# Routing and experts of a mixture-of-experts layer in one block, gate and up weights in four parts, the experts of a step packed in one integer

## What is computed

```python
g_idx = argmax(h @ w_group_router + b)            # one group per token
top_l, top_i = top_k(expert logits of that group, 2)
weights = p_g * softmax(top_l)
hidden = silu(h @ w_exp_gate[e]) * (h @ w_exp_up[e])
y += (hidden * weight) @ w_exp_down[e]            # for the token's 2 experts
x = x + gate2 * y ; out = rms_norm(x)
```

## Time and profile before

| | us |
|---|---|
| median of 3 runs (lowest, highest) | 1262.19 (1260.89, 1267.14) |
| the profiled execution | 1268.32 |
| its span, first to last instruction | 1266.5 |
| PE busy | 1106.8 (87%) |
| DVE busy | 580.6 (46%) |
| ACT busy | 428.6 (34%) |
| POOL busy | 228.4 (18%) |
| HBM read and written | 382.85 MB, 39.24 MB |

### The profile page before, as it was taken

One profiled execution on the slowest core, in us unless ns is written; L12 is line 12 of the kernel. 1 busy time (PEld: TensorE's weight loads), 2 busy tenths in 40 slices (PEclk: granted clock), 3 DMA queues, 4 the chain that ended last, 5 costly groups with the idle time before them and its releaser, 6 DMA issues. The chain is left out here.

```text
span 1266.5 us, 19400 instructions
## 1 busy us (share of the span) xinstructions
PE 1106.8 (87%) x7006; PEld 799.0 (63%) x7006; DVE 580.6 (46%) x1031; ACT 428.6 (34%) x853; POOL 228.4 (18%) x163
## 2 busy tenths in 40 slices
PE   4799999988999895988999799985899579799874
PEld 1587777767999795988888688885333123233241
DVE  0763554105456686777776376654111111111147
ACT  2651211113333772666667455520111001011112
POOL 0000000012000583467765000000100000000050
PEclk9899999999999997999999799987899889999978
DMA  9437676512200726254320533227577945757375
GB/s 354 145 115 252 219 259 223 177 45 72 55 1 1 185 74 157 37 124 103 85 67 1 186 100 104 97 68 276 206 242 233 324 167 194 273 163 237 134 259 205
DMA packets 126845, 196.87 MB, mean 155 GB/s; under 512 B 19504, under 2 KB 92112, under 8 KB 124702
## 3 DMA queue, kind: packets, MB, share of 16 engines
q1 hardware_dynamic: 116108, 162.22, 40.1%
q0 software_dynamic: 5760, 20.97, 4.9%
q10 hardware_dynamic: 4882, 12.44, 2.5%
HBM read 382.85 MB, written 39.24 MB: 333 GB/s over the span
## 5 line engine op out<-in xcount | busy, mean ns | idle before, releaser
L2145 PE MATMUL moe_gu_ps<-moe_wgu,moe_xT 128*32 128x512 f32 x1408 | 164.7, 609 | 25.2 <-DMA moe_wgu<-in_w_exp_up 24.6
L2145 PEld LDWEIGHTS moe_gu_ps<-moe_wgu,moe_xT 128*32 128x32 f32 x1408 | 45.7, 112 | 125.3 <-issue 124.2
L96 PE MATMUL proj_acc_ps<-proj_w_hi,hidden_hT_hi 128*128 128x512 f32 x288 | 117.5, 408 | 7.5 <-DVE hidden_hT_lo L91 7.5
L98 PE MATMUL proj_acc_ps<-proj_w_hi,hidden_hT_lo 128*128 128x512 f32 x288 | 114.3, 397 | 0.0
L97 PE MATMUL proj_acc_ps<-proj_w_lo,hidden_hT_hi 128*128 128x512 f32 x288 | 113.9, 396 | 0.0
L1322 POOL TENSOR_TENSOR att_e<-att_e 128x1152 f32<-128x1152 f32 (+1 forms) x36 | 86.0, 2389 | 72.9 <-DVE att_e L1402 72.9
L1340 ACT ACTIVATE att_e<-att_sc_ps,att_shift 128x1152 f32<-128x1152 f32 (+1 forms) x72 | 81.5, 1132 | 40.6 <-DVE att_shift L1391 40.4
L2167 PE MATMUL moe_y_ps<-moe_wd,moe_hidT 128*32 128x512 f32 x704 | 84.3, 621 | 11.4 <-issue 10.6
L1391 DVE TENSOR_REDUCE att_shift<-att_sc_ps 128x1 f32<-128x1152 f32 (+1 forms) x72 | 86.2, 1231 | 5.5 <-PE att_sc_ps L1436 5.5
L1465 PE MATMUL att_turned_ps<-att_in_v_tok,att_aT 128*128 128x128 f32 x584 | 76.9, 279 | 8.1 <-ACT att_aT L1348 8.1
L1465 PEld LDWEIGHTS att_turned_ps<-att_in_v_tok,att_aT 128*128 128x128 f32 x584 | 69.8, 191 | 13.7 <-ACT att_aT L1348 10.5
(11 more groups left out here) (372 smaller groups left out, 2102.3 us busy)
## 6 DMA issues: line engine op xcount, KB each, us to landing
moe_wgu<-in_w_exp_gate SPq DMA_DIRECT2D x178, 512.0 KB
moe_wgu<-in_w_exp_up SPq DMA_DIRECT2D x178, 512.0 KB
moe_wd<-in_w_exp_down SPq DMA_DIRECT2D x89, 1024.0 KB
scratch_y_slots<-moe_y ACTq DMA_DIRECT2D x22, 512.0 KB, 5.4
proj_raw<-in_w_in SPq DMA_DIRECT2D x32, 256.0 KB, 4.8
proj_feat<-in_w_ada SPq DMA_DIRECT2D x4, 2048.0 KB, 8.9
proj_xh<-in_w_ada SPq DMA_DIRECT2D x4, 2048.0 KB, 9.5
proj_feat<-in_w_ada SPq DMA_DIRECT2D x4, 1024.0 KB, 5.9
```

The costliest lines, as they stand in the source:

```text
L96: pe.matmul(out, a_high, b_high, start=start, stop=False)
L98: return pe.matmul(out, a_low, b_high, start=False, stop=stop)
L2145: mm = pe.matmul(gu_ps[n % 2][at, :], xT[:, n % 2, k * P + c * Q:k * P + (c + 1) * Q], wgu[:, c, k], start=(k == 0), stop=(k == KT - 1))
```

## The change

1. Routing and experts share one block and one scope for semaphores. The barrier between them and ACT's wait for the last h2 tile are gone; POOL waits for the token list (`tokens_done`) and the h2 tile (`h2_in`) before its first gather. To have room for both, the routing uses the experts' PSUM tiles and its one-hot matrices lie in the experts' `y` and `xT`; `xg` has two buffers instead of three.
2. Gate and up are loaded, waited for and released in four parts of 2 row tiles (256 KB a load) instead of two halves. The number of matmuls and their order are the same.
3. The codes of the four streams of a step are packed in one integer (5 bits each) by DVE; SP loads that once per step and takes experts and flags apart in registers, which are kept (`snap`).

```diff
+PARTS = 4
-def load_gate_up(sp, I, W, c, half, e, **cond):
-    rows = slice(half * (KT // 2), (half + 1) * (KT // 2))
+def load_gate_up(sp, I, W, c, part, e, new):
+    rows = slice(part * KT // PARTS, (part + 1) * KT // PARTS)
...
-def weights_of(eng, W, c, step):
-    n = c * STEPS + step
-    code = eng.value_load(W["block_weights"][0:1, n:n + 1], min_val=0, max_val=2 * NE - 1)
-    return code & (NE - 1), code >= NE
+def weights_of(eng, W, step):
+    code = eng.value_load(W["step_weights"][0:1, step:step + 1], min_val=0, max_val=(2 * NE) ** STREAMS - 1)
+    codes = [(code >> (5 * c)) & (2 * NE - 1) for c in range(STREAMS)]
+    return [(eng.snap(v & (NE - 1)), eng.snap(v >= NE)) for v in codes]
...
+        oh_place = [rows[:, 0:T * P].rearrange("p (t n) -> p t n", t=T) for rows in (spare_y, spare_x)]
+        x_ps, (rank_ps, sum_ps), table_ps, unread_ps = W["x_ps"], W["gu_ps"], W["h_ps"], W["y_ps"]
...
-            firsts = [weights_of(sp, W, c, 0) for c in range(STREAMS)]
-            for half in range(2):
-                sp.wait_ge(W["gu_in"][half], 16 * 2)
+            firsts = weights_of(sp, W, 0)
+            for part in range(PARTS):
+                sp.wait_ge(W["gu_in"][part], 16 * 2)
...
-            act.wait_ge(W["h2_in"], 16)
...
-            dve.scalar_tensor_tensor(out=W["block_weights"][0:1, :], in0=fresh[:]..., scalar=float(NE), in1=of_block[:]..., ...)
+            dve.scalar_tensor_tensor(out=codes[:], in0=fresh[:], scalar=float(NE), in1=of_block[:], op0=ALU.mult, op1=ALU.add)
+            dve.drain()
+            for c in range(STREAMS - 2, -1, -1):
+                dst = codes[:, c] if c else W["step_weights"][:]
+                op = dve.scalar_tensor_tensor(out=dst, in0=codes[:, c + 1], scalar=2.0 * NE, in1=codes[:, c], op0=ALU.mult, op1=ALU.add)
+                if c:
+                    dve.drain()
+            op.then_inc(blocks_done, 1)
...
-            dve.tensor_copy(W["step_token"][:], table_ps[:, 0:STEPS])
+            dve.tensor_copy(W["step_token"][:], table_ps[:, 0:STEPS]).then_inc(W["tokens_done"], 1)
...
-    XB = 3
+    XB = 2
...
+                now, ahead = ahead, weights_of(sp, W, n) if n < STEPS else []
+                for part in range(PARTS):
+                    sp.wait_ge(gu_done[part], n)
...
+            pool.wait_ge(W["tokens_done"], 1)
+            pool.wait_ge(W["h2_in"], 16)
...
-                pe.wait_ge(gu_in[half], gu_loaded(n))
-                for k in range(half * (KT // 2), (half + 1) * (KT // 2)):
+                for part in range(half * PARTS // 2, (half + 1) * PARTS // 2):
+                    pe.wait_ge(gu_in[part], gu_loaded(n))
+                    for k in range(part * KT // PARTS, (part + 1) * KT // PARTS):
...
+                    mm.then_inc(gu_done[part], 1)
...
-        routing_stage(nc, I, C, W, M)
+            block = moe_ctx.enter_context(nc.Block())
+            routing_stage(nc, I, C, W, M, block)
+            expert_stage(nc, I, C, W, M, block)
         late_ctx.close()
-        expert_stage(nc, I, C, W, M)
```

More of the change, by code:

```diff
@@ L2083, in expert_stage @@
         x_turned, x_left, x_right = s.sem("x_turned"), s.sem("x_left"), s.sem("x_right")
-        gu_done, silu_done, hid_done = [s.sem(f"gu_done{half}") for half in range(2)], s.sem("silu_done"), s.sem("hid_done")
+        gu_done, silu_done, hid_done = [s.sem(f"gu_done{part}") for part in range(PARTS)], s.sem("silu_done"), s.sem("hid_done")
         h_turned, hidT_done, d_done = s.sem("h_turned"), s.sem("hidT_done"), s.sem("d_done")
         y_left, y_right, y_out = s.sem("y_left"), s.sem("y_right"), [s.sem(f"y_out{u}") for u in range(2)]
-        block = ctx.enter_context(nc.Block())
         token, weight = W["step_token"], W["step_weight"]
@@ L2101, in _ @@
             for n in range(1, STEPS + 1):
-                now, ahead = ahead, [weights_of(sp, W, c, n) for c in range(STREAMS)] if n < STEPS else []
-                for half in range(2):
-                    sp.wait_ge(gu_done[half], n)
+                now, ahead = ahead, weights_of(sp, W, n) if n < STEPS else []
+                for part in range(PARTS):
+                    sp.wait_ge(gu_done[part], n)
                     for c, (e, new) in enumerate(ahead):
-                        load_gate_up(sp, I, W, c, half, e, cond=new)
+                        load_gate_up(sp, I, W, c, part, e, new)
                 if now:
@@ L2109, in _ @@
                 for c, (e, new) in enumerate(now):
-                    load_down(sp, I, W, c, e, cond=new)
+                    load_down(sp, I, W, c, e, new)
             load_final_gains(sp, I, W, M)
@@ L2446, in build @@
         W["final_in"] = e.sem("final_in")
-        W["gu_in"], W["d_in"] = [e.sem(f"gu_in{half}") for half in range(2)], e.sem("d_in")
+        W["gu_in"], W["d_in"], W["tokens_done"] = [e.sem(f"gu_in{part}") for part in range(PARTS)], e.sem("d_in"), e.sem("tokens_done")
         W["wgu"], W["wd"] = e.sb("wgu", [P, STREAMS, KT, 2 * FF]), e.sb("wd", [P, STREAMS, 2, D])
-        routing_stage(nc, I, C, W, M)
+        with ExitStack() as moe_ctx:
+            W["moe_scope"] = scope = Scope(nc, moe_ctx, "experts")
+            W["xT"], W["y"] = scope.sb("xT", [P, 2, KT * P]), scope.sb("y", [P, 2, D])
+            W["x_ps"], W["gu_ps"], W["h_ps"], W["y_ps"] = scope.ps("x", D), [scope.ps(f"gu{u}") for u in range(2)], scope.ps("h"), scope.ps("y", D)
+            block = moe_ctx.enter_context(nc.Block())
+            routing_stage(nc, I, C, W, M, block)
+            expert_stage(nc, I, C, W, M, block)
         late_ctx.close()
-        expert_stage(nc, I, C, W, M)
         final_stage(nc, I, C, W, M)
```

64 lines of the change are left out of this document (30 added, 34 removed).

## The result

The changed kernel takes 1268.8 us (median of 20 runs, 1264.0 to 1273.4) against 1264.1 us for the kernel before beside it (20 runs): ratio 1.0036 with the interval 1.0022 to 1.0050. That is 4.7 us more where 9.4 less were forecast, and above the range's end at 1264. (The forecast was reckoned from 1262.2, the median of the first 3 runs of before; from the 1264.1 of 20 runs it would be 1254.7.) A ratio here is the time against that of the kernel before in the same batch of runs. It leaves out single executions that took far longer than the others, such as one of 1339.1 us in parts4_unpacked and one of 2208.2 in ups_act4, while the medians have them in. The profiled execution took 1267.5 us (span 1265.6).

A forecast was written before the change was run, and what follows sets the result against it. PE was taken as the bound, busy for 87% of the span, with idle time mostly from up-weight loads. Seam 6.7 plus expert stage 2.7 gave 9.4 us off 1262.2, so 1252.8 us, range 1241 to 1264.

The forecast's parts named there:

- What bounds the kernel, and the seam: PE busy 87% of the span; between routing and experts, dropping the barrier gains 6.7 us (4.5 to 8).
- Rival (d): The seam gives little, as h2, first gather or first weights land late: 1257.5 us; chance 0.10.
- SP's list of a clean step: SP's issuing in a step without a new expert takes 10.4 us, under PE's 11.68.
- rival (c): Slower: SP becomes the bound of every step, about 1284 us, or 1270 at half the excess; chance 0.07.
- What PE gets: Expert stage with four parts: when loads land against PE's need; gain 2.7 us, bounds +10 and -6.
- steps 3 to 5: Three successive steps with one new expert each: stalls of 4.7 us instead of 3.4, a loss of 1.3.
- step 8 (to 10): All four streams take a new expert, bound by bytes: gain 3.1 us; 7.7 us wait before down stays.
- step 13 (to 15): Two streams take a new expert: issue-bound in part 3, SP's lag costs 0.5 us at down weights; zero.
- steps 18, 19 (and 20): Single new experts: step 18's 2.4 us stall goes, step 19 costs 1.6; gain about 0.9 us.
- (b): Same seam, but SP's lag eats more than the parts give: stage -4, 1259.5 us; chance 0.15.
- (a): SP's work hidden, single stalls vanish, steps 8 and 13 each lose 3.6 us: 1243 us; chance 0.20.
- (e): Quarter loads stream more slowly, say 308 instead of 385 GB/s: 1261 us; chance 0.04.

The follow-up runs named there:

- parts4_unpacked: The changed kernel, still with four parts, but the packing undone (one integer per stream and step, four register loads on SP): 1280.4 us, ratio 1.0103.
- ups_act4: The changed kernel with four parts, the expert stage's up loads issued from ACT's queue instead of SP's: 1252.5 us, ratio 0.991.
- parts8: The changed kernel with eight parts (128 KB a load) instead of four: 1447.4 us (one run).
- before_b: A second profile of the kernel before the change, no edit: 1260.5 us.
- known4: The changed kernel (four parts) with this data's schedule of real expert loads written in, no codes read or skipped loads: 1247.1 us, ratio 0.9849.
- known2: The changed kernel with halves instead of quarters and this data's schedule of real expert loads written in: 1250.6 us, ratio 0.9892.

## Why the prediction was wrong, step by step

**What bounds the kernel, and the seam: right.** Predicted was a gain of 6.7 us; measured are 8.4 at the first transposes, 0.5 of it because the routing began earlier (848.6 against 849.1), and 6.9 to 7.8 up to the first down product. The h2 store went back by 0.24 us, 0.7 from the routing's start, as predicted for the packing, and PE needed 6.70 us from POOL's gather to the transposes instead of 7.49. The token list came at 874.76, later than planned, and cost nothing, since the h2 tile landed last. The first weights were in time. Rival (d) is out.

**SP's list of a clean step: right.** Predicted 10.4 us; the same items as measured give 0.57 + 4 x 0.76 + 12 x 0.52 + 0.55 = 10.4, and parts8 bears the terms out. The unpacking lies elsewhere, though: not in one lump ahead of the first part but spread over its four pairs. Steps without a new expert stayed at 11.7, and rival (c) is out. The sum is not all that a turn takes, though. Two turns of SP that have nothing new, and in which it waits for nothing, took 11.2 us from down loads to down loads (954.62, 965.84, 977.04). Of the 0.8 us above the sum 0.3 is the down load of the expert before, a real one, and the rest lies in short gaps that nothing here explains.

**What PE gets: this step failed.** The forecast had a gain of 2.7 us in the stage; measured were -11.1 (-13.6 against the second profile). The mechanism, SP's lag, was right. The terms for it were too small (how far SP falls behind with new experts, how fast it recovers), and slower matmuls behind a wait were put at nothing outside step 8. By the forecast's terms (gains positive):

| term | predicted | measured | against before_b |
|---|---|---|---|
| steps 3 to 5 | -1.3 | -4.4 | -3.8 |
| step 8 (to 10) | +3.1 | +0.4 | -2.1 |
| step 13 (to 15) | 0 | -2.7 | -3.1 |
| steps 18, 19 (and 20) | +0.9 | -4.4 | -4.5 |

Three sizes were off, all in the same direction. First, I let SP start each chain of steps without a lag. In fact it was late before step 3: it issues without a pause from 904 on (19 pairs from 904.3 to 916.8) and begins the pairs of step 3 at 912.3, where the plan, counted from PE's start at 909.0, had it through with the codes at 911.2. Part 3 was then issued 6.7 us after it was free; the plan had 4.6 for its pair. Nor did SP recover as planned: its two turns behind step 5 took 11.2 us where the plan had 10.4, so it made up 0.5 us in each and not 1.3, and the first load of step 8 was issued 3.7 us after PE's start on step 7 (978.91, 975.25) instead of 2.5. Second, a real load was priced at its issue time on a queue with room, 13.7 us for a turn with one new expert. The turns of steps 3, 4 and 5 took 13.9, 15.5 and 14.4; single issues took longer, 2.10 us at 934.38 and 1.42 at 1146.39. Why isn't shown: the DMA engines were only 0.41 busy from 934 to 936, and ACT had issued its store of y at 934.10, but other loads beside a store took 0.4 us. Third, I priced a wait at its own length, other than in step 8. This is the largest of the three: the matmuls of the two products are busy for 6.2 us more (6.6 against the second profile) of the 13.8 between forecast and result. A stretch at 1.2 GHz can come with a wait: ahead of this down product PE waits 0.69 and then 2.06 us, and the 32 matmuls take 1.7 us more.

```profile
1170.41 5.34 PE L2177 MATMUL experts_y_ps<-moe_wd,experts_hidT 128*32 128x512 f32 x32 [2.06 <-issue]
```

It ends step 19, and it waits for the down weights of step 18, which stand behind 16 pairs in SP's queue: the lag is paid there. The granted clock is 0.50 of 2.4 GHz from 1172 to 1174. Behind the wait of 2.77 us at 944.27 it stays at 1.00, so this term is not the same for each wait. The stall of step 18, which the forecast had gone (2.40 us), is 1.23. In step 8 the parts did land one by one. PE's timeline of after:

```profile
989.95 3.57 PE L2155 MATMUL experts_gu_ps<-moe_wgu,experts_xT 128*32 128x512 f32 x16 [2.84 <-DMA moe_wgu<-in_w_exp_up]
997.08 3.51 PE L2155 MATMUL experts_gu_ps<-moe_wgu,experts_xT 128*32 128x512 f32 x16 [3.56 <-DMA moe_wgu<-in_w_exp_up]
...
1009.24 3.64 PE L2155 MATMUL experts_gu_ps<-moe_wgu,experts_xT 128*32 128x512 f32 x16 [4.68 <-DMA moe_wgu<-in_w_exp_up]
```

The waits add up to less than the 10.25 + 4.14 of before, but each is followed by 16 matmuls of 3.5 to 3.6 us at the low clock (granted 0.50 or 0.51 from 990 to 993, 998 to 1000 and 1009 to 1012), where 1.9 are needed at the high one. The forecast had one slow stretch of 16 matmuls behind the last landing; there are three. The wait of 7.7 us ahead of the down product behind them stayed, as forecast (7.64). known4 gets 3.3 us more out of the same parts, not much above the scatter of these steps, so that SP had its share here too is likely and not shown.

**The rivals.** (b) was right in kind: SP's lag ate more than the parts gave, in the steps that it named and with the down product as the place. It had 0.15 and a stage of -4; the size was -11 to -14. The lower bound of -6 for the stage (1 us in each of 6 steps) was the term that should have been wider: a lag that SP recovers at 0.5 us in a clean step is not gone after one or two, and three steps in a row each start from the lag of the last. (a) is in part what known4 shows, with SP's list taken away (stage 273.0): the single stalls go, but its 3.6 us in step 13 do not come (45.4 against 45.2 and 44.8). (e) is out. The Trainium skill's rule (DMA: Bandwidth & Descriptors, section Bandwidth) for loads of at least 1 MiB pointed to the right sign. The Trainium skill's figures in that section are of DMAs issued from GpSimd, while the loads here are issued from SP, and lower throughput isn't what is at work here: known4 with 256 KB loads is not slower than known2 with 512 KB. What small loads cost here is the issuing engine's time, and more stretches at the low clock.

## What to carry over

Before splitting transfers, count what the issuing queue does in a loop's turn, skipped issues and register work included, and compare it with the turn: a spare of 1.3 us in 11.7 by the sum, 0.5 as measured, was not enough, since a turn with real loads goes over it and the lag falls on whatever stands last in the queue. Price a wait on TensorE with the slow stretch that may follow it. And take the parts of a change one by one: here the seam (6 to 8 us) pays, the packing pays only for the quartering, and the quartering pays only once its issues are spread over two queues.

## What the runs showed of the hardware

A DMA that its condition skips still costs its queue 0.07 us, and a gate and up pair 0.52 us with its address arithmetic, in parts8 as in halves. A real load of 256 KB occupies SP for 0.38 to 0.46 us, as one of 512 KB does; now and then a single issue took longer, 2.10 us at 934.38. Loads of 256 KB moved at 383 GB/s in step 8, those of 512 KB at 385. TensorE's clock fell to 1.2 GHz behind waits of 0.69 and 2.06 us in step 19, and stayed at 2.4 behind one of 2.77 us in step 4.
